# Matmuls of 512 columns written as two of 256 in one output projection of a decoder trunk

## The reference

```python
def gla_mixer(h, w_in, w_gate2, b_gate, g_norm, w_out):
    ...                                   # chunked scan over 64 tokens
    o = rms_norm(o, g_norm) * jax.nn.silu(g_out.reshape(B, S, H, dv))
    return o.reshape(B, S, H * dv) @ w_out

def reference(x, ...):
    h = x
    for i in range(DEPTH):                # DEPTH = 2: GLA, then gMLP
        y = rms_norm(h, norm_mix[i])
        ...
        h = h + y
        h = h + swiglu(rms_norm(h, norm_ffn[i]), w_ffn_gate[i], w_ffn_up[i], w_ffn_down[i])
    return rms_norm(h, norm_final)
```

## Time and profile before

| what | value |
|---|---|
| median of three runs | 2529.44 us |
| span of the profiled execution (first to last instruction) | 2527.5 us |
| TensorE busy in the span | 2495.3 us, 99%, 11632 matmul records |
| TensorE weight loads busy | 2073.8 us, 82%, 11632 records |
| DVE, ACT, POOL busy | 69%, 44%, 51% |
| mean granted TensorE clock | 0.999 of full speed |
| phase "ao" | from 408.2 to about 490.8 us, 336 matmuls |

### The profile page before, as it was taken

One profiled execution on the slowest core, in us unless ns is written; L12 is line 12 of the kernel. 1 busy time (PEld: TensorE's weight loads), 2 busy tenths in 40 slices (PEclk: granted clock), 3 DMA queues, 4 the chain that ended last, 5 costly groups with the idle time before them and its releaser, 6 DMA issues.

```text
span 2527.5 us, 33336 instructions
## 1 busy us (share of the span) xinstructions
PE 2495.3 (99%) x11632; PEld 2073.8 (82%) x11632; DVE 1744.5 (69%) x2233; ACT 1101.0 (44%) x1955; POOL 1292.2 (51%) x980
## 2 busy tenths in 40 slices
PE   8999999999999999999999999999999999999998
PEld 6787888778888888888888888888887888888887
DVE  5255678868778665578665999965666877656556
ACT  4344555543333344465344333444544333334444
POOL 3234556555555555454666455544455555555543
PEclk9999999999999999999999999999999999999999
DMA  7674426246666568654987555596634655326764
GB/s 238 211 263 153 112 82 226 97 143 210 211 215 217 175 200 286 193 193 131 335 318 235 171 166 172 180 348 222 196 105 150 225 200 204 125 71 220 268 191 150
DMA packets 311258, 493.37 MB, mean 195 GB/s; under 512 B 32992, under 2 KB 132704, under 8 KB 311104
## 3 DMA queue, kind: packets, MB, share of 16 engines
q1 hardware_dynamic: 311104, 491.39, 58.0%
HBM read 328.24 MB, written 154.66 MB: 191 GB/s over the span
## 4 chain that ended last, share of the span: by engine, by line
PE 51%; DVE 1%; ACT 1%; DMA 1%; issue 0%; POOL 0%; SPq 0%; ACTq 0%; DVEq 0%
PE ps L682 16%; PE ps L684 16%; PE ps L683 16%; PE ps L2821 2%; PE ps L2677 0%; DMA t_scratch<-n_all 0%; DMA stg<-in_b_w_in 0%; DVE r_all L1978 0%; POOL ring_lo L758 0%; ACT ring_hi L754 0%; DVE r_all L1973 0%; ACT junk L1513 0%; DVE xl_all L1936 0%; POOL r_all L1333 0%; DVE r_all L1929 0%
## 5 line engine op out<-in xcount | busy, mean ns | idle before, releaser
L758 POOL TENSOR_TENSOR ring_lo<-stg,ring_hi 128x512 fp32r<-128x512 f32 x666 | 955.8, 1438 | 890.3 <-ACT ring_hi L754 889.6
L754 ACT ACTIVATE ring_hi<-stg 128x512 fp32r<-128x512 f32 x666 | 420.0, 631 | 1029.8 <-PE ps L684 902.0
L682 PE MATMUL ps<-xh_all,ring_hi 128*128 128x512 f32 x1536 | 600.0, 391 | 0.3 <-issue 0.3
L684 PE MATMUL ps<-xh_all,ring_lo 128*128 128x512 f32 x1536 | 597.8, 389 | 0.0
L683 PE MATMUL ps<-xl_all,ring_hi 128*128 128x512 f32 x1536 | 597.6, 389 | 0.0
L776 DVE TENSOR_TENSOR s_ring<-s_stage,s_ring 128x512 fp32r<-128x512 f32 x238 | 299.4, 1271 | 219.0 <-ACT s_ring L772 218.7
L682 PE MATMUL ps<-ring_hi,s_ring 128*128 128x512 f32 x1064 | 415.3, 390 | 0.7 <-issue 0.5
L684 PE MATMUL ps<-ring_hi,s_ring 128*128 128x512 f32 x1064 | 414.1, 389 | 0.0
L683 PE MATMUL ps<-ring_lo,s_ring 128*128 128x512 f32 x1064 | 414.0, 389 | 0.0
L682 PEld LDWEIGHTS ps<-xh_all,ring_hi 128*128 128x128 f32 x1536 | 288.4, 188 | 60.4 <-issue 1.5
L684 PEld LDWEIGHTS ps<-xh_all,ring_lo 128*128 128x128 f32 x1536 | 288.3, 188 | 60.3
(11 more groups left out here) (274 smaller groups left out, 3628.6 us busy)
## 6 DMA issues: line engine op xcount, KB each, us to landing
s_stage<-h_scratch SPq DMA_DIRECT2D x238, 256.0 KB, 3.4
stg<-t_scratch SPq DMA_DIRECT2D x200, 256.0 KB, 3.5
h_scratch<-r_all SPq DMA_DIRECT2D x34, 1024.0 KB, 5.1
h_scratch<-r_all SPq DMA_DIRECT2D x80, 256.0 KB, 3.4
stg<-in_w_ffn_gate SPq DMA_DIRECT2D x34, 512.0 KB, 4.4
stg<-in_w_ffn_up SPq DMA_DIRECT2D x34, 512.0 KB, 5.8
stg<-in_w_ffn_down SPq DMA_DIRECT2D x66, 256.0 KB, 3.5
t_scratch<-r_all SPq DMA_DIRECT2D x28, 512.0 KB, 3.0
```

The source lines that it names most:

```text
L682: pe.matmul(bank, s_hi, m_hi, start=first, stop=False, skip_group_check=more)
L684: return pe.matmul(bank, s_lo, m_hi, start=False, stop=last, skip_group_check=more)
L754: nc.scalar.activation(weight_slot(ring_hi, g), weights(g), ACT.Copy).then_inc(wh_done, 1)
L758: nc.gpsimd.tensor_tensor(weight_slot(ring_lo, g), weights(g), f32(weight_slot(ring_hi, g)), ALU.subtract).then_inc(wl_done, 1)
```

## The change

In phase "ao" alone the call of `product` is replaced by the new helper `product_in_halves`. For each of the three combinations it writes two matmuls of 256 columns, one for each half of the bank, with the same stationary operand. The flag `start` (which begins an accumulation in the bank) stands on the first of the six matmuls only. The semaphore increments after the last matmul are as before. "d0", "go" and "d1", the other calls of `d_phase`, still use `product`.

```diff
+        def product_in_halves(pe, bank, s_hi, s_lo, m_hi, m_lo, first, last):
+
+            for s_, m_ in ((s_hi, m_hi), (s_hi, m_lo), (s_lo, m_hi)):
+                for c in (slice(0, BANK // 2), slice(BANK // 2, BANK)):
+                    mm = pe.matmul(bank[:, c], s_, m_[:, c], start=first and m_ is m_hi and s_ is s_hi and c.start == 0,
+                                   stop=last and s_ is s_lo, skip_group_check=True)
+            return mm
...
-                            mm = product(pe, ps[:, first_bank + t, :], s_slot(g, 0)[:, tile(t)], s_slot(g, 1)[:, tile(t)],
-                                         w_ring(ring_hi, g), w_ring(ring_lo, g), j == 0 and q in (1, 2, 3, 7),
-                                         j == pairs - 1, q in (6, 5, 4))
+                            if name == "ao":
+                                mm = product_in_halves(pe, ps[:, first_bank + t, :], s_slot(g, 0)[:, tile(t)],
+                                                       s_slot(g, 1)[:, tile(t)], w_ring(ring_hi, g), w_ring(ring_lo, g),
+                                                       j == 0 and q in (1, 2, 3, 7), j == pairs - 1)
+                            else:
+                                mm = product(pe, ps[:, first_bank + t, :], s_slot(g, 0)[:, tile(t)], s_slot(g, 1)[:, tile(t)],
+                                             w_ring(ring_hi, g), w_ring(ring_lo, g), j == 0 and q in (1, 2, 3, 7),
+                                             j == pairs - 1, q in (6, 5, 4))
```

## The result

The changed kernel takes 2536.90 us (median of 7 runs, 2535.13 to 2538.48), the kernel before 2529.44 us (7 runs beside them, 2528.32 to 2532.08). The ratio is 1.0024, with a 95% interval of 1.0015 to 1.0033: slower. The predicted time was 2533.0 us with a range of 2528.6 to 2537.5. Later comparisons put the kernel before at a median of 2530.3 to 2530.8 us, about 1 us above this first one, and the changed kernel at 2536.70, so the loss is 6 to 7.5 us.

A forecast was written before the change was run, and what follows sets the result against it. The prediction took TensorE as the bound: 336 added matmuls cost +4.5 us, waits near the end of "ao" give back 0.9, so +3.6 us on 2529.4 makes 2533.0 us, range 2528.6 to 2537.5.

The forecast's parts named there:

- another mechanism, a distance near 125 ns: Rival in "ao": load becomes the bound with the excess on top, or an issue limit; +6.5 us, 2535.9 us; chance 0.17.
- The bound: TensorE, busy 99% of the span; "ao" costs its time on TensorE plus the few waits in it.
- The fixed cost, p = 120.1 ns: Distance between 256-column matmul starts in "ao", with 13.4 ns a cost of each float32r instruction; growth 4.5 us.
- The 2.5 ns and 0.8 us: Estimate from the skill page: 2.5 ns of its own per matmul, so the split in "ao" would add 0.8 us.
- the rival of a free split: In "ao" the 13.4 ns go with columns or hide beside the load; 2528.3 to 2530.9 us; chance 0.22.
- The load limit, 111.6 ns: In "ao" loads of 128 columns allow starts 111.6 ns apart, below 120.1, so they do not bind the halves.
- No overlap: Rival in "ao": closely following loads don't overlap matmuls, 228 ns each; about 2604 us; chance 0.06 with other large losses.
- the rule that the prediction cited: Skill page: weight loads overlap matmuls in flight only when their row group differs; cited for the no-overlap rival.
- What is given back, -0.9 us: Near the end of "ao", slower TensorE uses up waits for VectorE: 0.46 us before the transposes, at most 0.48 at "f0".

The follow-up runs named there:

- the small delay: The kernel before with four of the 512-column matmuls at the start of "ao" issued twice, no halves: 2532.83 us, ratio 1.0008.
- loops exchanged: The changed kernel with the helper's two loops exchanged, three matmuls for the left half of the bank, then three for the right: 2537.22 us.
- the uneven split: The changed kernel with each matmul split at 384 and 128 columns instead of 256 and 256: 2548.01 us.

## Why the prediction was right, and where it was short

**The number: inside the range, and partly by luck.** The forecast was +3.6 us, within +1.5 to +5; measured is +7.5 us, about twice that, and 0.6 us below the upper end of the range. That end was there for another mechanism, a distance near 125 ns with 2535.9 us and up to 2538, and the distance was 120.0 ns. So the cost of the matmuls was right, and what else came on top was not foreseen.

**The bound: right.** Added work on TensorE in "ao" came out in the time, whether as halves or as full matmuls.

**The fixed cost, p = 120.1 ns: right.** Measured 120.0, and the term of 4.5 us is 4.48 in the trace. The doubt was whether the 13.4 ns at 512 columns are a rate or a cost per instruction, since before only one length existed. The distance at 256 columns settles it: 226.7 - 120.0 = 106.7 ns for 256 columns leaves no room for a slower rate. The 2.5 ns and 0.8 us that the prediction set beside its own estimate did not come true. In the rival of a free split the sum was misworked: p from 111.6 to 114.6 ns gives -1.2 to +0.8 us, not +2.7.

**The load limit, 111.6 ns, beside and not on top: right.** It came from the plain float32 matmuls of the earlier trace rows, and the kernel with four of 128 columns shows 111.7 ns for float32r (by the load, or by an issue limit of that size).

**No overlap: excluded,** and with it the rule that the prediction cited for it from the Trainium skill, "TensorE: Matmul & The Clock Gate", section "The mechanism". Even at a distance of 111.7 ns there is a load for each matmul; a load of about 108 ns and 53.3 ns of columns one after the other would need 161 ns.

**What is given back, -0.9 us: this is the step that failed.** In its place stands nothing: "ao" grew by 4.5 us, the full cost of its matmuls. The wait at "f0" did vanish, -0.48 us. But the waits before the transposes grew by 0.67 us where they should have shrunk by 0.46. The prediction took VectorE's chain as fixed from its last stop at 467.68 us on the earlier trace rows. What it left out is GpSimd. This is POOL in the kernel before, and then VectorE and POOL in the changed one, at the same instructions:

```profile
467.72 1.81 POOL L758 TENSOR_TENSOR ring_lo<-stg,ring_hi 128x512 fp32r<-128x512 f32 x1
```

```profile
471.33 1.55 DVE L784 TENSOR_TENSOR s_ring<-y_t,s_ring 128x512 fp32r<-128x512 f32 x1 [1.41 <-ACT s_ring L780]
...
471.04 1.30 POOL L766 TENSOR_TENSOR ring_lo<-stg,ring_hi 128x512 fp32r<-128x512 f32 x1
```

Before, VectorE started 0.04 us ahead of POOL, took 0.69 us, and POOL's operation took 1.81. Now POOL starts 0.29 us ahead and takes 1.30, and VectorE's takes 1.55. Whichever comes second is drawn out until the other is through. This isn't a matter of two rows: in the trace of before, 178 of VectorE's 266 L776 began while one operation of POOL was running and met no other, and all of them ended 0.54 to 0.61 us after that operation's end; with nothing on POOL beside it, L776 took 0.68 us.

VectorE lost 0.86 us by it, and TensorE waits for VectorE here. The kernels with halves up to the end of the phase all have VectorE at 1.55 us, the kernel with extra full matmuls has 1.37; the one with halves in the first four sub-products, the one with the small delay and the kernel before have 0.69. What puts POOL first is argued: steps of 2.88 us in place of 2.72 let POOL, which has other work to fill in, get ahead. No run moved POOL's operation alone. The second wait grew by 0.28 us as VectorE's next operation did, from 2.11 to 2.40 us, with POOL's L766 starting 0.04 us after it; why it is drawn out here and not before is not shown:

```profile
479.45 2.40 DVE L1937 SCALAR_TENSOR_TENSOR r_all<-r_all,stats,gain_bc 128x1024 f32<-128x1024 f32 x1
```

**The low clock: missing from the sum.** The waits of 2.4 us, one in each feed-forward, stand in the groups by line of the kernel before, over the whole span, as 4.8 us of idle time before the transposes; the prediction looked at "ao" alone:

```profile
L2677 PE MATMUL ps<-ident,r_all 128*128 128x128 f32 x208 | 27.6, 274 | 7.1 <-DVE xl_all L1936 4.8 <-DVE r_all L1929 1.9 <-DVE r_all L1973 0.5
```

Behind the first of them the low clock is in all seven traces of kernels with a delay of 4.5 us or more that kept the wait, over 3 to 9 matmuls of 512 columns. Of the four with less or no delay it is in two. Behind the second, which is as long, it is in none of the eleven. In two traces (loops exchanged, four of 128) the clock was also low near 220 us, behind a wait of 1.8 us that is 1.0 us in the first trace of before.

It is no property of the halves: over 75 runs of the kernel before, those with a mean clock of 0.999 took 2529.2 us on average (20 runs), with 0.998 2530.9 us (40 runs), with 0.997 2532.6 us (15 runs). The 13 runs of the changed kernel had 0.996 to 0.998, never 0.999; its six with 0.998 took 2535.7 us on average, 4.8 us over the like of before. So the 6 to 7.5 us of the medians are 4.5 us of "ao" and some 1.5 to 3 us that go with the clock and with which runs were drawn; which of these a run gets is partly chance. With the 4.5 us of delay a full mean clock is rarer: 1 run in 30 of the changed, the exchanged and the extra-matmul kernels, against 20 in 75 of the kernel before. Why is not shown and stays open.

## What to carry to other kernels

In this kernel a float32r matmul of N columns cost N / 2.4 + 13.3 ns at 512 and 256 columns, and 111.7 ns in a row of 128-column ones, each with a load of 128 columns; so split a 512-column matmul in two only for a gain of more than 13 ns. Where one engine is full, a change of a few microseconds is still moved by several tenths wherever it meets a wait for a second engine that shares its path with a third: look for the place where the bound engine idles, also outside the phase that is changed. Taking away one such idle of 2.5 us in each of two phases was worth more here (6.2 us) than the whole change cost in matmul time (4.5 us).

## What was not expected of the hardware

- Float32r matmuls of 128 columns come every 111.7 ns in a row, where the limit of the loads was put; in the uneven split the next matmul started 58 to 61 ns after one of 128 columns, so there is no sign of a lower rate for short ones.
- After TensorE had been idle for 2.4 us between 524.3 and 526.7 us, its granted clock was at the 1.2 GHz level for the next microseconds, in 9 of 11 traces with this wait, which cost 1.5 us in the changed kernel's trace. After a wait of the same length near 1910 us it was full in all of them.
- VectorE and GpSimd, in elementwise operations on two operands in SBUF, took turns: 0.69 us became 1.55 us for the one that started 0.29 us later.
